# Two transformer blocks on one core: how the second block's input norm gets its sums, and how its first two tiles are multiplied

## The reference

```python
# end of first_block
f = (jax.nn.silu(h @ w_ffn_gate[l]) * (h @ w_ffn_up[l])) @ w_ffn_down[l]
x = x + rms_norm(f, norm_ffn_post[l])
# start of second_block
h = rms_norm_2(x, norm1_g[l])
z = h @ w_in[l]
a, gate, q, k, v = jnp.split(z, splits, axis=-1)
...
def rms_norm_2(x, g):
    xf = x.astype(jnp.float32)
    y = xf * lax.rsqrt(jnp.mean(xf * xf, axis=-1, keepdims=True) + EPS)
    return (y * g.astype(jnp.float32)).astype(x.dtype)
```

## Time and profile before

| what | value |
| --- | --- |
| time, median of 3 runs | 1456.29 us (1455.47 to 1456.39) |
| the profiled execution | 1456.94 us |
| its span, first to last instruction | 1455.2 us, mean granted clock 0.999 |
| TensorE busy | 1444.2 us (99%), 7020 matmuls |
| VectorE, ScalarE, GpSimd busy | 677.4, 585.4, 653.8 us |
| mean DMA rate | 92 GB/s |
| chain that ended last | PE 74%, issue 14%, DVE 5%, POOL 4%, ACT 1% |

### The profile page before, as it was taken

The page is one execution under the profiler, slowest core; times in us unless marked ns, Lnnn a source line. Parts: engine busy times, 40 slices in busy tenths (PEclk is TensorE's granted clock), DMA queues, the critical chain, the costliest instruction groups (busy, mean ns, idle before and its releaser), DMA issues.

```text
span 1455.2 us, 19531 instructions
## 1 busy us (share of the span) xinstructions
PE 1444.2 (99%) x7020; PEld 1171.3 (80%) x7020; DVE 677.4 (47%) x1093; ACT 585.4 (40%) x922; POOL 653.8 (45%) x304
## 2 busy tenths in 40 slices
PE   9999999999999999999999999999999999999999
PEld 6888888788788778888888887777678888888887
DVE  6426656775525285333331018989664333333000
ACT  5243435665643253332232225666654223222221
POOL 4434324762244434444444452766134444444443
PEclk9999999999999999999999999999999999999999
DMA  5422211111133223233233333322122223323333
GB/s 188 148 88 87 87 58 58 45 59 59 46 100 101 96 78 96 93 101 99 89 101 101 114 103 131 102 65 66 45 76 99 96 92 101 100 88 101 105 111 118
DMA packets 38573, 134.15 MB, mean 92 GB/s; under 512 B 4496, under 2 KB 4752, under 8 KB 38512
## 3 DMA queue, kind: packets, MB, share of 16 engines
q1 hardware_dynamic: 37248, 130.70, 27.5%
q10 hardware_dynamic: 1264, 2.62, 0.6%
HBM read 131.20 MB, written 2.10 MB: 92 GB/s over the span
## 4 chain that ended last, share of the span: by engine, by line
PE 74%; issue 14%; DVE 5%; POOL 4%; ACT 1%; DMA 0%; POOLq 0%; SPq 0%; DVEq 0%
PE bank L1177 18%; PE bank L1178 18%; PE bank L1179 18%; POOL wL L497 4%; PE bank L1530 3%; PE bank L1532 2%; PE bank L1531 2%; PE bank L1206 1%; PE bank L1208 1%; PE bank L1207 1%; PE bank L1309 1%; PE bank L1307 1%; PE bank L1308 1%; DVE bank L2291 1%; PE bank L1585 1%
## 5 line engine op out<-in xcount | busy, mean ns | idle before, releaser
L497 POOL TENSOR_TENSOR wL<-raw,wH 128x1024 fp32r<-128x1024 f32 x234 | 574.1, 2453 | 745.6 <-ACT wH L593 620.5
L593 ACT ACTIVATE wH<-raw 128x1024 fp32r<-128x1024 f32 x209 | 221.3, 1059 | 586.5 <-PE bank L1179 520.4
L1177 PE MATMUL bank<-aH,wH 128*128 128x512 f32 x920 | 359.5, 391 | 0.4 <-POOL wL L497 0.4
L1179 PE MATMUL bank<-aH,wL 128*128 128x512 f32 x920 | 358.0, 389 | 0.0
L1178 PE MATMUL bank<-aL,wH 128*128 128x512 f32 x920 | 358.0, 389 | 0.0
L1177 PEld LDWEIGHTS bank<-aH,wH 128*128 128x128 f32 x920 | 172.7, 188 | 38.7 <-issue 1.0
L1178 PEld LDWEIGHTS bank<-aL,wH 128*128 128x128 f32 x920 | 172.7, 188 | 36.2 <-issue 0.5
L1179 PEld LDWEIGHTS bank<-aH,wL 128*128 128x128 f32 x920 | 172.7, 188 | 35.8
L1179 PE MATMUL bank<-fH,wL 128*128 128x512 f32 x352 | 137.0, 389 | 0.0
L1178 PE MATMUL bank<-fL,wH 128*128 128x512 f32 x352 | 137.0, 389 | 0.0
L1177 PE MATMUL bank<-fH,wH 128*128 128x512 f32 x352 | 136.9, 389 | 0.0
(11 more groups left out here) (346 smaller groups left out, 1995.4 us busy)
## 6 DMA issues: line engine op xcount, KB each, us to landing
raw<-in_w SPq DMA_DIRECT2D x234, 512.0 KB, 3.3
bmk<-in_bias SPq DMA_DIRECT2D x6, 512.0 KB, 4.7
out_x<-xT SPq DMA_DIRECT2D x8, 256.0 KB, 3.6
xT<-in_x SPq DMA_DIRECT2D x3, 512.0 KB, 8.2
ct<-in_ct ACTq DMA_DIRECT2D x3, 384.0 KB, 3.7
xT<-in_x SPq DMA_DIRECT2D x2, 256.0 KB, 4.3
raw<-in_w SPq DMA_DIRECT2D x2, 256.0 KB, 4.7
w1k<-in_w1k ACTq DMA_DIRECT2D x1, 512.0 KB, 4.4
```

The lines of the kernel that those rows point to most:

```text
L497: pool.tensor_tensor(wL[:, c_slot, :], raw[:, c_slot, :], wH[:, c_slot, :].bitcast(F32), ALU.subtract).then_inc(sem("w_lo"), 1)
L593: act.activation(wH[:, s, :], raw[:, s, :], ACT.Copy).then_inc(sem("w_hi"), 1)
L1177: pe.matmul(bank[:], hi, H[:, ka, :], start=(k == 0), stop=False)
L1179: mm = pe.matmul(bank[:], lo, H[:, ka, :], start=False, stop=(k == p.k - 1))
```

## The change

**Sums ahead.** With r the post-norm's root, g its gain and z the `dn1` output, the new x is x + r g z, so its sum of squares for a token is sum(x^2) + 2 r sum(g z x) + r^2 sum(g^2 z^2). While `dn1` still runs, VectorE accumulates `squares_of_z` (in the buffer `nt_`) and `products_with_x` (in `nr`) for tiles 0 to 6; for the last tile it forms z * x into `sq[:, 0]` and then copies the bank. `nx` still holds the mean of x^2 of block 1's second norm, for every token. TensorE forms five groups of sums of four one-column matmuls each (`side_sums`), one ahead of `spread_root(2)` and four behind it, where `idle_products` stood. After its fourth residual tile VectorE puts the three sums together (five linked 128x4 instructions), ScalarE takes Ln and Exp of 128x4 after its fifth tile, VectorE does Newton's step behind the last residual, TensorE spreads the root (`spread_root(3, B[4])`), and ScalarE copies it to `nr`. The squares of x, `add_up` and the wide root are gone.

**Opening.** Tiles 0 and 1 are done together: for each k four high products, and from k = 2 on the two low products of k - 2; the low products of k = 6 and 7 stand behind the spread.

**Low parts.** GpSimd makes `aL = tmp - aH`, where ScalarE writes both `aH` and the plain product `tmp`. VectorE's residual product goes to two PSUM banks instead of `tmp`.

**Third chunk.** Since the chunks of tiles 0 and 1 are now held until both are done, the high and low parts of tile 2's chunk get a place of their own (`third_hi`, `third_lo`, in `mH`), and are made right after `dn1`.

```diff
@@ gpsimd
-            pool.wait_ge(sem("ffn1_done"), 1)
+            pool.wait_ge(sem("w_hi"), i2 + 3)
+            pool.tensor_tensor(third_lo, raw[:, i2 % 2, :], third_hi.bitcast(F32), ALU.subtract).then_inc(sem("w_lo"), 1)
+            for kt in range(KD):
+                pool.wait_ge(sem("h3_hi"), kt + 1)
+                pool.wait_ge(sem("h3_x"), kt + 1)
+                pool.tensor_tensor(aL[:, kt, :], tmp[:, kt % 2, :], aH[:, kt, :].bitcast(F32), ALU.subtract)\
+                    .then_inc(sem("h3_lo"), 1)
+            pool.wait_ge(sem("res2"), KD)
@@ scalar
-            high_of_x("h3", "g_norm1", "res2", 4, True)
+            act.activation(third_hi, raw[:, p.c0 % 2, :], ACT.Copy).then_inc(sem("w_hi"), 1)
+            for kt in range(KD):
+                act.wait_ge(sem("res2"), kt + 1)
+                act.activation(aH[:, kt, :], xT[:, kt, :], ACT.Copy, scale=vec("g_norm1", kt)).then_inc(sem("h3_hi"), 1)
+                if kt >= 2:
+                    act.wait_ge(sem("h3_lo"), kt - 1)
+                act.activation(tmp[:, kt % 2, :], xT[:, kt, :], ACT.Copy, scale=vec("g_norm1", kt)).then_inc(sem("h3_x"), 1)
+                if kt == 4:
+                    act.wait_ge(sem("side_ready"), 4)
+                    act.activation(side_log, root_x, ACT.Ln).then_inc(sem("ln_ready"), 1)
+                    act.wait_ge(sem("ln_ready"), 5)
+                    act.activation(side_guess, side_log, ACT.Exp, scale=-0.5).then_inc(sem("nr_ready"), 1)
+            act.wait_ge(sem("root_spread"), 3)
+            act.activation(nr[:], B[4][:], ACT.Copy).then_inc(sem("nr_ready"), 1)
...
-            rsqrt(5, B[6][:], D, (sem("sum_ready"), 5), nr[:], B[5][:])
@@ tensor
             total_with_last(4 * KD, B[4])
-            idle_products(1)
+            pe.wait_ge(sem("side_ready"), 1)
+            side_sums(side_squares, sq[:, 1, :], squared_gains[:, KD - 1:KD], True)
             spread_root(2, B[5])
-            idle_products(2)
+            pe.wait_ge(sem("side_ready"), 3)
+            side_sums(side_squares, squares_of_z, ones[:, 0:1])
+            side_sums(side_mean, nx, ident[:, 0:1])
+            side_sums(side_products, products_with_x, ones[:, 0:1])
+            side_sums(side_products, sq[:, 0, :], vec("g_ffn_post", KD - 1)).then_inc(sem("sum_ready"), 1)
...
+            for k in range(KD):
                 high_products(k)
                 if k >= 2:
+                    pe.wait_ge(sem("h3_lo"), k - 1)
+                    for t in range(2):
+                        low_product(t, k - 2)
+            spread_root(3, B[4])
+            for t in range(2):
+                for k in range(KD - 2, KD):
+                    pe.wait_ge(sem("h3_lo"), k + 1)
+                    mm = low_product(t, k)
+                mm.then_inc(sem("chunk_done"), 1)
@@ vector
-            residual_and_low(z2T, "g_ffn_post", "res2", "h3", "g_norm1", 2, True)
-            dve.wait_ge(sem("res2"), KD)
-            dve.sem_inc(sem("ffn1_done"), 1)
-            norm(5, B[6], B[5])
+            dve.wait_ge(sem("root_spread"), 2)
+            for kt in range(KD):
+                dve.scalar_tensor_tensor(residual_bank(kt)[:], z2T[:, kt, :], vec("g_ffn_post", kt), B[5][:], ALU.mult, ALU.mult)\
+                    .then_inc(sem("res2_mul"), 1)
+                dve.wait_ge(sem("res2_mul"), kt + 1)
+                dve.tensor_tensor(xT[:, kt, :], residual_bank(kt)[:], xT[:, kt, :], ALU.add).then_inc(sem("res2"), 1)
+                if kt == 3:
+                    dve.wait_ge(sem("sum_ready"), 5)
+                    link(dve.tensor_tensor(root_x, side_squares, root, ALU.mult))
+                    link(dve.scalar_tensor_tensor(root_x, side_products, 2.0, root_x, ALU.mult, ALU.add))
+                    link(dve.tensor_tensor(root_x, root_x, root, ALU.mult))
+                    link(dve.scalar_tensor_tensor(root_x, root_x, 1.0 / D, side_mean, ALU.mult, ALU.add))
+                    dve.tensor_scalar(root_x, root_x, EPS, None, ALU.max).then_inc(sem("side_ready"), 1)
```

More of the change, by code:

```diff
@@ L312, in two_blocks_kernel @@
             up = up_[:, :, 0:S + 2 * HP]
+        third_hi, third_lo = (mH[:, 2 * i:2 * i + 2, :].rearrange("p a s -> p (a s)") for i in range(2))
         def slot_of(kind, n):
@@ L336, in narrow, with residual_bank @@
             return bank[:, 0:TT]
+        squares_of_z, products_with_x = nt_, nr
+        side_squares, side_products, side_mean, side_log, side_guess = (B[6][:, TT * i:TT * (i + 1)] for i in range(5))
+        def residual_bank(kt):
+            return B[(PH["in2"].t0 + 2 + kt % 2) % NBANK]
         def cst(name):
@@ L1051, in _ @@
                     head_roots_wide(SPREAD_AT[t])
-                ahead(p, t - 1)
+                if t > 1:
+                    ahead(p, t - 1)
                 if t - 1 in VALUES_AT:
@@ L1616, in values, with high_products @@
                 mm.then_inc(sem("na_pv"), 1)
-            bank0, bank1 = (B[(p.t0 + t) % NBANK] for t in range(2))
-            s0, s1 = (p.c0 % 2, (p.c0 + 1) % 2)
-            pe.wait_ge(sem("w_lo"), p.c0 + 1)
-            pe.wait_ge(sem("bank_free"), p.t0 + 1)
-            for k in range(KD):
+            opening = [(B[(p.t0 + t) % NBANK], (p.c0 + t) % 2) for t in range(2)]
+            def high_products(k):
                 b = slice(k * P, (k + 1) * P)
                 pe.wait_ge(sem("h3_hi"), k + 1)
-                pe.matmul(bank0[:], wH[:, s0, b], aH[:, k, :], start=(k == 0), stop=False, skip_group_check=True)
-                pe.matmul(bank0[:], wL[:, s0, b], aH[:, k, :], start=False, stop=False, skip_group_check=True)
-                add_up(k)
@@ L1640, in _, with low_product @@
+            def low_product(t, k):
+                bank, c_slot = opening[t]
+                return pe.matmul(bank[:], wH[:, c_slot, k * P:(k + 1) * P], aL[:, k, :], start=False, stop=(k == KD - 1),
+                                 skip_group_check=True)
             pe.wait_ge(sem("w_lo"), p.c0 + 2)
             pe.wait_ge(sem("bank_free"), p.t0 + 2)
-            low_products(range(KD - 3))
-            for k in range(2):
+            for k in range(KD):
                 high_products(k)
-            low_products(range(KD - 3, KD)).then_inc(sem("chunk_done"), 1)
@@ L1646, in _ @@
-            for k in range(KD):
                 if k >= 2:
-                    high_products(k)
-                mm = pe.matmul(bank1[:], wH[:, s1, k * P:(k + 1) * P], aL[:, k, :], start=False, stop=(k == KD - 1), skip_group_check=True)
-            mm.then_inc(sem("chunk_done"), 1)
+                    pe.wait_ge(sem("h3_lo"), k - 1)
[7 more added lines that the diff above has]
+                mm.then_inc(sem("chunk_done"), 1)
```

102 lines of the change are left out of this document (69 added, 33 removed).

## The result

The changed kernel took 1458.34 us (median of 19 runs, 1456.92 to 1459.48) beside 1455.72 us for the kernel before in the same session (19 runs, 1454.16 to 1458.06). The ratio on record is 1.0013, 95% interval 1.0007 to 1.0019: slower by some 1.9 us (the two medians as they stand lie 2.6 us apart), where 1.7 us less had been forecast. The profiled execution took 1458.97 us (span 1456.9).

A forecast was written before the change was run, and what follows sets the result against it. TensorE, busy 99% of the span, was taken to bind; side sums at half clock and eight slow products left a gain of 1.7 us from the median 1456.29, so 1454.5 us, range 1451.0 to 1456.6.

The forecast's parts named there:

- The seam: Between `dn1`'s last product and `in2`'s tile 2: side sums end at 880.5, tile 2 starts at 893.4, gain 1.7 us.
- a slow stretch of 12 to 16 products: In `in2`'s opening: that many products at half clock, or a busy VectorE, leave gain 0 to 1 us; chance 0.12.
- rival A: Side sums on TensorE: same cost at either clock, or the clock holds; gain 5.0 us, time 1451.3; chance 0.24.
- The small instructions: Five linked 128x4 VectorE instructions after the fourth residual pair: 1.0 us, plus 0.6 for one held by GpSimd.
- Behind it: After tile 2 of `in2`: sigmoid and first gated product 0.8 us later, taken up by the second; whole gain lasts.
- two SBUF inputs: VectorE beside a working GpSimd: an instruction with both inputs in SBUF waits, 0 to 1.3 us, taken as 0.6.
- Rival D: In `in2`: slow products or a busy VectorE hand 0.8 us lateness to TensorE; gain 0 to 1, near 1455.8; chance 0.12.
- a shift that shrinks through `in2`: Stages after tile 2: the sign for gain 0 to 1 us, where the forecast had all later stages shifted by one amount.

The follow-up runs named there:

- the version of the kernel before: The kernel before with its copy by column made three times instead of once; 1459.74 us, ratio 1.0026 to the kernel before.

## Why the prediction was wrong

**The seam: right in mechanism and size.** Forecast were sums at 0.22 us a pair, their end 10.75 us behind the token sums, eight slow products, a gain of 1.7. The trace shows 0.213, 10.64, seven, and 1.90. TensorE bound, as said. The residual ran at 1.39 us a pair out of PSUM and GpSimd held none of its sixteen long instructions. It was luck in one respect: the forecast gave "a slow stretch of 12 to 16 products" a small chance, but the same seam had a stretch of 10.2 us in three executions of four with these sums, and of 13.7 in the fourth (seam 25.06). Of rival A's two conditions the first is refuted: a one-column pair cost 0.213 us at half clock and 0.115 at full. The rule of the Trainium skill for a weight load (TensorE: Matmul & The Clock Gate, LDWEIGHTS), which has no term for the clock, doesn't fit these rows. Its second, that the clock holds, was not met by this kernel; where other sums met it, the seam was 21.73 us, and 19.70 with the small instructions freed.

**The small instructions: half right.** Only "one of them" was taken to be open to a hold. The last, with a single source, took 1.06 us; it lay under TensorE's slow products and cost nothing here, but 1.15 us once the clock held. The one with two sources was held in six of the versions (0.57 to 1.14) and not in the changed kernel (0.16 at 879.59), where it met the gap between two of GpSimd's instructions (about 879.63 to 879.74).

**The step that failed is "Behind it".** It said that VectorE comes 0.8 us later against tile 2, that the second gated product takes this up, and that "The whole gain should last to the end". Counted from tile 2, the eviction of tile 3 was 2.6 us late and not 0.8. Of this, 0.9 is the forecast lateness (the eviction of tile 2 at 6.82 us behind the start of tile 2 against 5.89), and it is indeed taken up: in the kernel with the copy from the bank VectorE's 1.0 us left tile 6 only 0.14 later. The other 1.7 is the third VectorE instruction there, which the prediction passed over: the copy of nr by column, at nothing in its sum. It took 0.62 us before and 2.31 once the new seam had moved it against GpSimd's low halves, and it came out on TensorE as a wait of 1.82 us. The prediction's rule for a hold was "two SBUF inputs", and the copy has one. The rows show such copies at 2.31, 2.32 and 2.71 us, and small instructions with one source at 1.06 to 1.17; with the source in a bank the copy took 0.68 beside the same GpSimd instruction. The same line of the Trainium skill (GPSIMD Engine Reference, Key points) names a second kind beside the two sources, VectorE's instructions in a two-port mode, and the prediction left it out. That single-source instructions are held agrees with it; that these ran in such a mode no row shows.

**What wasn't priced at all** is what a late VectorE sets off in `in2`: ScalarE's queue holds the chunk's high half behind the sigmoid, GpSimd's holds the low half behind two taps, and the chain had ended just in time before (917.02 for a tile that could have begun at 916.9). Those rows were in the trace of before. Nor was the price of a gap: TensorE's 1.8 us of waiting are followed by 3.4 us at half clock in this execution of the changed kernel. Rival D had the right place, and its sign of being wrong, a shift that shrinks through `in2`, is what the trace shows; but it let the loss end at the size of the gain.

**The sum, put right:** -1.9 (seam) + 1.7 (wait, net) + 1.7 (slow stretch behind it) = +1.5, beside +1.45 at the first sums of the heads and +1.9 by the ratio of the runs.

The middle term stands in every trace of this chain (waits of 1.82, 1.84 and 1.82 us); the last does not. With the sums 64 columns wide the same wait was followed by full clock (a wait of 1.82 at 915.24, granted clock 1.00 until 996), and so was the longer one in the version of the kernel before; with the sums among the products it was followed by 3.4 us at half. How often the changed kernel has this stretch is open. A mean of 0.995 or less means at least 13 us at half clock (0.0045 of 1457 us, twice; an estimate), so each of the 19 runs had more than the 10.2 us of the seam, here or elsewhere. When exactly the clock falls and returns is open too: the same instructions gave 10.2 and 13.7 us.

## What to carry to other kernels

When a change moves engines against each other, list every instruction on VectorE that lies near a GpSimd instruction, single-source copies from SBUF to SBUF included, and ask of each what is queued behind it, in the other engines too; reading the source from a PSUM bank, where it is still there, frees it. Don't count one-column products as work that keeps TensorE's clock up: in all five traces with these sums and no idle products among them it fell for 10.2 or 13.7 us, as it did with a TensorE that waited in their place, and in the three with 64 columns it held through the sums. The wider ones cost next to nothing here (0.90 us for eight at 64 columns). And before taking out products that "do nothing", ask what clock the work behind them will get.

## What the runs showed of the hardware that was not expected

- One-column pairs took 0.10 to 0.115 us at 2.4 GHz and 0.195 to 0.213 at 1.2 GHz; with 64 columns 0.105 to 0.12 at 2.4 GHz.
- A 128x4 `tensor_scalar` from SBUF to SBUF took 0.16 to 0.17 us with GpSimd idle and 1.06 to 1.17 beside it; from a bank 0.16 beside GpSimd.
- After the same instructions the clock stayed at 1.2 GHz for 10.2 us in some executions and 13.7 in others; a seam without the pairs, waiting in their place, had 10.2 as well.
- The mean granted clock of a run hints at such stretches: 0.994 to 0.995 in all 19 runs of the changed kernel, 0.998 to 1.000 with sums 64 columns wide and the copy from the bank, 0.996 to 0.999 with the wide sums alone.
